# Splitting the bias, key and value loads of a chunk-band attention over two blocks of a program, and moving two state stores

## The chip, the cores and the metric

The kernel runs on one core of a Trainium2 chip. The metric is the device time of one launch in microseconds. A launch computes one whole inference step: 1024 prompt frames and 8 sample requests of 16 frames, nine tiles of 128 rows in all.

## What is computed

The step is one layer of a streaming encoder. A combined projection gives the queries, keys and values of two branches, and the gates. Branch A is a chunk-band softmax attention with a learned bias by relative distance; branch B is a retention with a recurrent state. They are merged, and a mixture of experts and an embedding follow. What the change touches is branch A for the prompt, and the updated retention states of the samples, which are outputs:

```python
def rel_bias_block(table, n_q, n_k, offset):
    dist = jnp.arange(n_q)[:, None] + offset - jnp.arange(n_k)[None, :]
    idx = jnp.clip(dist, -REL_CLIP, REL_CLIP) + REL_CLIP
    return table[:, idx].astype(F32)

def attend(q, k, v, bias, valid=None):
    s = jnp.einsum('bqhd,bkhd->bhqk', q, k).astype(F32) * (HEAD_DIM_A ** -0.5) + bias[None]
    ...
    p = jax.nn.softmax(s, axis=-1)
    return jnp.einsum('bhqk,bkhd->bqhd', p.astype(v.dtype), v)
...
    new_state = state * jnp.exp(log_g * T)[None, :, None, None] + jnp.einsum(
        'bjhd,bjhe->bhde', k * k_decay[None, :, :, None], v)
```

A prompt tile t of 128 queries sees its own 128 keys and up to 512 keys before it, so tile 0 uses one block of 128 keys, tile 1 two, and tiles 4 to 7 all five (`blocks(t)`). There are 8 heads.

## The kernel before

Everything is written out by hand: each engine has its own list of instructions, and semaphores tie them. `build` (L3112) makes two blocks of its own and one in `stage_ab`; at the end of a block all engines meet in a **barrier**. The change works around the first barrier, between the block of `stage_ab` (with `retain_samples`, L949) and the block that begins with `stage_c` (L1151).

The matmul work that does not depend on the attention is "hosted" in it (`Hosted`, L876): the gate columns of the projection, 6 panels of 512 columns for 9 tiles, which makes 54 **units** numbered u = 0 to 53. A unit is 8 slabs of 3 matmuls of 128x512 (`split_product`, L161 to L163). Its rows, 1 MiB, are loaded by `load_rows` (L913) when unit u-2 is done; its 256 KB result is evicted by ScalarE (L923) and stored (L918). Units 0 to 5 (`LEAD`, 48 slabs) run in the first block, beside the last part of the retention for the samples; unit 6 on, in the attention. There, a step n is one head of one prompt tile, n = 8t + h, and TensorE computes 6 slabs per step for n below 16 and 5 after that. A panel of the weights is 2 MiB: panel 1 is loaded whole (L893) in the first block, panel 2 in four pieces of 512 KB (L897) at n = 5, 6 and 7.

The order of DMA issues on SyncE (SP) is written in `retain_samples` (L993 to L1041) and in `stage_c` (L1244 on). Nearly all transfers of the kernel are issued there, on one queue. In the first block SP loads the kept keys `c.kT` (L1017, 9 tiles, 2.25 MiB), the values `c.vA` (L1018, 2.25 MiB) and the queries of tile 0 (L1019). Then it goes through u = 0 to 5. At u = 1 it loads the bias, 8 DMAs (L1033), each of 16 partitions x 8 heads x 640 columns, 320 KB. At u = 3 it stores four even sample states (L990, 512 KB each, through `states`). At u = 5 it waits until the even states have landed (`even_stored`), because panel 1 goes into their place, loads the panel, stores two of the odd states, and then loads the rows of unit 7. ScalarE stores the other two odd states after the eviction of unit 4. GpSimd (POOL) sets the two corners of the bias that the band excludes (L1067, L1069) when all of the bias has landed. The vector engine starts the attention with a wait for both (L1326), TensorE with a wait for keys and values (L1490).

Of the kernel before, what the change touches and what calls it, by code (L numbers as in the profile page):

```python
# [12 lines left out]
P = 128  # L13
D = 1024
KD = D // P
SEQ, DEC_B, DEC_S = 1024, 8, 16
PT = SEQ // P
NT = PT + 1
HA, HDA = 8, 64
# [929 lines left out]
def retain_samples(c, block, b):  # L949
# [8 lines left out]
    st_done = s.counter("st_done", HB)  # L958
    st_out = s.counter("st_out", DEC_B * HB)
    tables_in, states_in, even_stored, stored, bias_in = (c.sem(f"b2_{n}") for n in ("tables_in", "states_in", "even_stored", "stored", "bias_in"))  # L960
    c.kv_in, c.bias_ready = c.sem("kv_in"), c.sem("bias_ready")
    halves, raw = [c.at(R1 + 4 * 1024 * par, DEC_B // 2, HB, DV) for par in range(2)], c.at(R1 + 16 * 1024, KD, BANK)
    st = [halves[n % 2][:, n // 2] for n in range(DEC_B)]
    c.qz_in, = s.dmas("qz_in")
# [21 lines left out]
    def states(eng, par, some):  # L986
        for j in some:
            n = 2 * j + par
            eng.wait_ge(*st_out(0, 16 * par + 8 + 2 * j + 2))
            eng.dma_start(c.o["state_s"][n].rearrange("h d e -> d h e"), st[n]).then_inc(stored if par else even_stored, 16)  # L990

    @block.sync
    def _(sp):  # L993
        s.credit(sp)
# [19 lines left out]
        for stored_ in kv_stored:  # L1014
            sp.wait_ge(*stored_(NT - 1, 0))
            sp.wait_ge(*stored_(NT - 2, 1))
        sp.dma_start(c.kT, c.kT_kept).then_inc(c.kv_in, 16)  # L1017
        sp.dma_start(c.vA, c.o["v_all"].rearrange("t p n -> p t n")).then_inc(c.kv_in, 16)  # L1018
        sp.dma_start(c.qz_tiles[:, 0].rearrange("p h n -> p (h n)"), row(c.qz, 0)).then_inc(*c.qz_in.inc(0))  # L1019

        for u in range(LEAD // KD):
            if u == LEAD // KD - 1:
                sp.wait_ge(even_stored, 16 * DEC_B // 2)
                H.load(sp, 1)
                states(sp, 1, (0, 1))
            H.load_rows(sp, u + 2)
            if u < LEAD // KD - 1:
                H.store(sp, u)
            if u == 1:
                sp.wait_ge(b["state_stored"], 16)  # L1030
                sp.wait_ge(*b["kd_ready"](last))
                for q in range(DEC_B):
                    sp.dma_start(c.bias[q:P:DEC_B], bass.AP(tensor=c.skew.tensor, offset=P - 1 - q, ap=[  # L1033
                        [SKEW - DEC_B, DEC_S], [DEC_S * SKEW, HA], [1, NKB * P]])).then_inc(bias_in, 16)
            if u == 3:
                sp.wait_ge(*rb_ready(last))
                sp.dma_start(row(c.rb, NT - 1), rb.rearrange("p h n -> p (h n)")).then_inc(stored, 16)
                states(sp, 0, range(4))
# [17 lines left out]
    @block.gpsimd  # L1056
    def _(pool):
        pool.wait_ge(*proj_done(last, 4))
        nc.gpsimd.memset(qm, 0.0).then_inc(*km_ready.inc)
        pool.wait_ge(tables_in, 48)  # L1060
        for par in range(2):
            nc.gpsimd.tensor_tensor(km[:, par], kr.rearrange("p (h n) -> p h n", h=HB),
                                    kdec[:, par].unsqueeze(2).to_broadcast([P, HB, DK]), ALU.mult).then_inc(*km_ready.inc)
        pool.wait_ge(*ms_ready(last))
        nc.gpsimd.tensor_tensor(rstd, ms, c.half[:, 0:HB], ALU.pow).then_inc(*rstd_ready.inc)
        pool.wait_ge(bias_in, 16 * (P // DEC_S))
        nc.gpsimd.memset(c.bias[0:64, :, 576:], NEG).then_inc(c.bias_ready, 1)  # L1067
        pool.wait_ge(c.bias_ready, 1)
        nc.gpsimd.memset(c.bias[64:P, :, 0:64], NEG).then_inc(c.bias_ready, 1)  # L1069

    @block.vector
    def _(dve):
# [73 lines left out]


SCALE = HDA ** -0.5


def stage_c(c, block):  # L1151
# [29 lines left out]
    def blocks(t):  # L1181
        return min(t + 1, NKB)
# [61 lines left out]
    def _(sp):  # L1244
# [3 lines left out]
        def load_q(t):  # L1248
            sp.wait_ge(*s_done(t - 2))
            sp.dma_start(qz[:, t % 2].rearrange("p h n -> p (h n)"), row(c.qz, t)).then_inc(*qz_in.inc(t % 2))  # L1250

        H.store(sp, LEAD // KD - 1)
        load_q(1)

        def load_keys(n):
            sp.wait_ge(*kT_done(n - 2))
# [15 lines left out]
        for n, (t, h) in enumerate(steps):  # L1272
            if n and h == 0 and t + 1 < PT:
                load_q(t + 1)
            if n in (44, 52):
                load_keys((n - 44) // 8)
            if 8 <= n < 16:
# [39 lines left out]
    @block.gpsimd  # L1317
    def _(pool):
        nc.gpsimd.memset(zeros, 0.0).then_inc(zeroed, 1)
        nc.gpsimd.memset(cv[:, :, 2, :], 0.0).then_inc(values_padded, 1)  # L1320
        give_back(c, *past)
        F.ungated(pool)

    @block.vector
    def _(dve):
        dve.wait_ge(c.bias_ready, 2)  # L1326

        def head(t, h):
            n = blocks(t) * P
            dve.wait_ge(*s_done(t, h + 1))  # L1330
            dve.wait_ge(*p_ready(t, h - 1))
            two = lambda ap: ap.rearrange("p (a n) -> p a n", a=2)
            nc.vector.scalar_tensor_tensor(two(S[:, h % 2, 0:n]), s_halves(h, n // 2), SCALE, two(c.bias[:, h, NKB * P - n:]), ALU.mult,  # L1333
                                           ALU.add).then_inc(*s_out.inc)
# [154 lines left out]
    def _(pe):  # L1489
        pe.wait_ge(c.kv_in, 32)  # L1490

        def scores(t, f):
# [2 lines left out]
            k0, w = (t - (nb - 1)) * P, nb * P // 2  # L1495
            if f == 0:
                pe.wait_ge(*qz_in(t, t % 2))
            pe.wait_ge(*s_out(t, 2 * f))
            for part in range(2):
                for h in (2 * f, 2 * f + 1):  # L1500
# [1658 lines left out]
```

## Time and profile before

| | us |
|---|---|
| median of 3 runs | 1954.7 |
| the runs | 1951.64, 1954.7, 1957.15 |
| the profiled execution, its own time | 1951.89 |
| its span, first to last instruction | 1950.1 |
| TensorE (PE) busy | 1856.6, 95% |
| DVE, ACT, POOL busy | 1124.6, 841.5, 201.3 |

The profile is of one execution. It gives the busy time of each engine, the same in 40 slices of the span, the granted clock of TensorE, the busy share of the 16 DMA engines, and the chain of work that ended last. A busy share of a DMA window can come out above 1.00, since the packets of a transfer overlap. In the timeline a row gives the start in us, the duration, engine, line, operation and tiles; in brackets stands the idle time of the engine before it and what ended it. "SPq" rows are DMA issues of SyncE: their duration is the time of issuing, not that of the transfer.

### The profile page before, as it was taken

How to read it: one execution, taken by the hardware profiler on the slowest of the kernel's cores; microseconds unless marked ns; L12 is line 12 of the kernel's file. 1: busy time of each engine (PE TensorE's matmuls, PEld its weight loads, DVE VectorE, ACT ScalarE, POOL GpSimd, SP SyncE). 2: the span in 40 equal slices, each digit the busy share in tenths (PEclk: the TensorE clock that was granted, in tenths of full speed). 3: DMA queues.
4: the chain of work that ended last, by engine and by line, in shares of the span. 5: the costliest groups of instructions: out<-in, count | busy, mean ns of one | idle time of the engine just before them, and what ended most of it. 6: DMA issues, size and time to landing. Idle time of an engine off the chain costs nothing. (4 is left out here: it accounts for less than half of the span.)

```text
span 1950.1 us, 26441 instructions
## 1 busy us (share of the span) xinstructions
PE 1856.6 (95%) x9542; PEld 1517.9 (78%) x9542; DVE 1124.6 (58%) x1389; ACT 841.5 (43%) x1026; POOL 201.3 (10%) x235
## 2 busy tenths in 40 slices
PE   6999999998999999989999997899999999999598
PEld 5888888876777777767888886788888888888486
DVE  5344333343333445436445436689988998898674
ACT  4223000010343444435222213687778777877442
POOL 1000211120000000001322001100000000000220
PEclk9999999999999999999999998899999999999799
DMA  9656111179879766496334437599999999998762
GB/s 344 232 180 246 60 70 46 59 262 323 294 250 333 269 208 211 156 364 222 124 133 165 162 114 323 218 389 404 398 393 396 405 399 392 391 404 339 252 199 76
DMA packets 122271, 497.32 MB, mean 255 GB/s; under 512 B 17872, under 2 KB 33752, under 8 KB 99416
## 3 DMA queue, kind: packets, MB, share of 16 engines
q1 hardware_dynamic: 111360, 469.24, 64.8%
q0 software_dynamic: 7200, 18.88, 2.8%
q10 hardware_dynamic: 3640, 8.26, 1.1%
q8 instruction: 44, 0.72, 0.1%
q14 instruction: 27, 0.22, 0.0%
HBM read 411.53 MB, written 92.14 MB: 258 GB/s over the span
## 5 line engine op out<-in xcount | busy, mean ns | idle before, releaser
L2677 DVE TENSOR_TENSOR expert_w_rounded<-arena,expert_w_rounded 128x2048 fp32r<-128x2048 f32 x126 | 283.0, 2289 | 30.9 <-ACT expert_w_rounded L2612 28.9
L162 PE MATMUL psum<-expert_w_rounded,expert_x_rounded 128*128 128x512 f32 x640 | 250.0, 391 | 0.0
L2612 ACT ACTIVATE expert_w_rounded<-arena 128x2048 fp32r<-128x2048 f32 x126 | 233.9, 1911 | 0.0
L161 PE MATMUL psum<-expert_w_rounded,expert_x_rounded 128*128 128x512 f32 x504 | 202.1, 401 | 0.0
L163 PE MATMUL psum<-expert_w_rounded,expert_x_rounded 128*128 128x512 f32 x504 | 197.0, 391 | 0.0
L161 PE MATMUL psum<-host_w_rounded,host_x_rounded 128*128 128x512 f32 x432 | 177.3, 410 | 12.3 <-DMA host_x_rounded<-hx_scratch 6.8
L162 PE MATMUL psum<-host_w_rounded,host_x_rounded 128*128 128x512 f32 x432 | 171.0, 396 | 0.0
L163 PE MATMUL psum<-host_w_rounded,host_x_rounded 128*128 128x512 f32 x432 | 170.9, 396 | 0.0
L162 PEld LDWEIGHTS psum<-expert_w_rounded,expert_x_rounded 128*128 128x128 f32 x640 | 120.8, 189 | 23.4
L1333 DVE SCALAR_TENSOR_TENSOR arena<-psum,arena 128x640 f32<-128x640 f32 (+4 forms) x64 | 41.8, 653 | 167.5 <-PE psum L1502 167.5
L2612 ACT ACTIVATE first_gate_rounded<-arena 128x2048 fp32r<-128x2048 f32 x64 | 119.1, 1917 | 1.4 <-DMA arena<-w_down_e 1.4
L161 PE MATMUL psum<-b_w_rounded,b_x_rounded 128*128 128x512 f32 x288 | 115.2, 400 | 0.5 <-DVE b_w_rounded L434 0.5
L163 PE MATMUL psum<-b_w_rounded,b_x_rounded 128*128 128x512 f32 x288 | 112.3, 390 | 0.0
L162 PE MATMUL psum<-b_w_rounded,b_x_rounded 128*128 128x512 f32 x288 | 112.2, 389 | 0.0
L163 PEld LDWEIGHTS psum<-expert_w_rounded,expert_x_rounded 128*128 128x128 f32 x504 | 94.6, 188 | 20.5
L692 ACT ACTIVATE arena<-psum,arena 128x512 f32<-128x512 f32 x18 | 12.4, 689 | 224.9 <-PE psum L163 224.9
L161 PEld LDWEIGHTS psum<-expert_w_rounded,expert_x_rounded 128*128 128x128 f32 x504 | 95.2, 189 | 17.7
L161 PEld LDWEIGHTS psum<-host_w_rounded,host_x_rounded 128*128 128x128 f32 x432 | 83.0, 192 | 32.8 <-DMA host_x_rounded<-hx_scratch 9.3
L161 PE MATMUL psum<-first_gate_rounded,expert_x_rounded 128*128 128x512 f32 x264 | 104.4, 396 | 4.3 <-DVE expert_x_rounded L2683 4.3
L163 PE MATMUL psum<-first_gate_rounded,expert_x_rounded 128*128 128x512 f32 x264 | 103.9, 394 | 0.0
L161 PE MATMUL psum<-a_w_rounded,a_x_rounded 128*128 128x512 f32 x216 | 85.6, 396 | 17.5 <-DVE a_w_rounded L591 17.5
L163 PEld LDWEIGHTS psum<-host_w_rounded,host_x_rounded 128*128 128x128 f32 x432 | 82.6, 191 | 18.2
(321 smaller groups left out, 3832.0 us busy)
## 6 DMA issues: line engine op xcount, KB each, us to landing
arena<-w_gate_e SPq DMA_DIRECT2D x32, 2048.0 KB, 13.6
arena<-w_up_e SPq DMA_DIRECT2D x32, 2048.0 KB, 14.1
arena<-w_down_e SPq DMA_DIRECT2D x32, 2048.0 KB, 13.2
host_x_rounded<-hx_scratch SPq DMA_DIRECT2D x54, 1024.0 KB, 5.5
y_scratch<-arena SPq DMA_DIRECT2D x49, 512.0 KB, 11.9
z_scratch<-arena SPq DMA_DIRECT2D x54, 256.0 KB, 5.8
arena<-w_in SPq DMA_DIRECT2D x6, 2048.0 KB, 11.7
arena<-x_all SPq DMA_DIRECT2D x18, 512.0 KB, 6.0
```

The costliest lines, as they stand in the source:

```text
L161: nc.tensor.matmul(out, x_hi, w_hi, start=first, stop=False)
L162: nc.tensor.matmul(out, x_hi, w_lo, start=False, stop=False)
L163: return nc.tensor.matmul(out, x_lo, w_hi, start=False, stop=last)
L692: nc.scalar.activation(v[:, b, h * BANK:(h + 1) * BANK], ps[:, 2 + h, :], ACT.Copy, scale=row_rstd[:, b:b + 1]).then_inc(*bv_out.inc)
L1333: nc.vector.scalar_tensor_tensor(two(S[:, h % 2, 0:n]), s_halves(h, n // 2), SCALE, two(c.bias[:, h, NKB * P - n:]), ALU.mult, ALU.add).th ...
L2612: nc.scalar.activation(c.exact(his[0 if last_down(n, e) else n][:, half, :]), halves[b][n][:, half, :], ACT.Copy).then_inc(*w_hi_ready[n].inc)
L2677: nc.vector.tensor_tensor(c.exact(raw), raw, c.high(his[0 if last_down(n, e) else n][:, half, :]), ALU.subtract).then_inc(*w_lo_ready[n].inc)
```

## The change

It makes four edits.

- Keys and values are loaded in two parts by `load_kept`. The first block loads tiles 0 to 3 (`EARLY` = 4), 1 MiB each. Step n = 10 of the attention loads keys of tiles 4 to 8 (1.25 MiB) and values of tiles 4 to 7 (1 MiB). Tile 8 of the values is no longer loaded. TensorE waits for the second part at prompt tile 4.
- The bias is loaded in two parts by `load_bias`. The first block loads the last 256 of 640 columns (from `NEAR` = 384), 8 DMAs of 128 KB. The other 384 columns come one DMA per step at n = 0 to 7, 192 KB each.
- The two odd state stores of SP go behind the barrier, after the queries of tile 1.
- POOL's second corner is set in the second block, when all of the bias is in. DVE waits for the first corner at the start of the attention and for the second at prompt tile 2.

```diff
+    c.odd_states = states
...
-        sp.dma_start(c.kT, c.kT_kept).then_inc(c.kv_in, 16)
-        sp.dma_start(c.vA, c.o["v_all"].rearrange("t p n -> p t n")).then_inc(c.kv_in, 16)
+        load_kept(c, sp, 0, EARLY)
...
                 H.load(sp, 1)
-                states(sp, 1, (0, 1))
...
-                    sp.dma_start(c.bias[q:P:DEC_B], bass.AP(tensor=c.skew.tensor, offset=P - 1 - q, ap=[
-                        [SKEW - DEC_B, DEC_S], [DEC_S * SKEW, HA], [1, NKB * P]])).then_inc(bias_in, 16)
+                    load_bias(c, sp, q, NEAR, NKB * P)
...
-        pool.wait_ge(bias_in, 16 * (P // DEC_S))
+        pool.wait_ge(bias_in, 16 * DEC_B)
         nc.gpsimd.memset(c.bias[0:64, :, 576:], NEG).then_inc(c.bias_ready, 1)
-        pool.wait_ge(c.bias_ready, 1)
-        nc.gpsimd.memset(c.bias[64:P, :, 0:64], NEG).then_inc(c.bias_ready, 1)
...
+EARLY, NEAR = 4, (NKB - 2) * P
+
+
+def load_kept(c, eng, t0, t1):
+
+    eng.dma_start(c.kT[:, :, t0 * P:t1 * P], c.kT_kept[:, :, t0 * P:t1 * P]).then_inc(c.kv_in, 16)
+    t1 = min(t1, PT)
+    eng.dma_start(c.vA[:, t0:t1], c.o["v_all"][t0:t1].rearrange("t p n -> p t n")).then_inc(c.kv_in, 16)
+
+
+def load_bias(c, eng, q, n0, n1):
+
+    eng.dma_start(c.bias[q:P:DEC_B, :, n0:n1], bass.AP(tensor=c.skew.tensor, offset=P - 1 - q + n0, ap=[
+        [SKEW - DEC_B, DEC_S], [DEC_S * SKEW, HA], [1, n1 - n0]])).then_inc(c.bias_in, 16)
...
         load_q(1)
+        c.odd_states(sp, 1, (0, 1))
...
+            if n < DEC_B:
+                load_bias(c, sp, n, 0, NEAR)
+            if n == 10:
+                load_kept(c, sp, EARLY, NT)
...
         nc.gpsimd.memset(cv[:, :, 2, :], 0.0).then_inc(values_padded, 1)
+        pool.wait_ge(c.bias_in, 32 * DEC_B)
+        pool.wait_ge(values_padded, 1)
+        nc.gpsimd.memset(c.bias[64:P, :, 0:64], NEG).then_inc(c.bias_ready, 1)
...
-        dve.wait_ge(c.bias_ready, 2)
+        dve.wait_ge(c.bias_ready, 1)
...
+            if (t, h) == (2, 0):
+                dve.wait_ge(c.bias_ready, 2)
...
+                if t == EARLY:
+                    pe.wait_ge(c.kv_in, 64)
```

How this moves the issues on SP is seen at two places. The first is SP around the barrier, from the load of panel 1 (`w_in`, L893) on. L913 loads the rows of a unit, L918 stores a unit's result, L436 is the end of the first block. Before:

```order
L893 DMA arena<-w_in 128x8x512
L990 DMA state_s<-arena 128x4x256 x2
L913 DMA host_x_rounded<-hx_scratch 128x2048
L436 UNCONDITIONAL_BRANCH
L1243 UNCONDITIONAL_BRANCH
L918 DMA z_scratch<-arena 128x512
L1250 DMA arena<-qz_scratch 128x1024
L913 DMA host_x_rounded<-hx_scratch 128x2048
```

Now:

```order
L893 DMA arena<-w_in 128x8x512
L913 DMA host_x_rounded<-hx_scratch 128x2048
L436 UNCONDITIONAL_BRANCH
L1256 UNCONDITIONAL_BRANCH
L918 DMA z_scratch<-arena 128x512
L1263 DMA arena<-qz_scratch 128x1024
L990 DMA state_s<-arena 128x4x256 x2
L1160 DMA arena<-bias_skew_scratch 16x8x384 x2
L913 DMA host_x_rounded<-hx_scratch 128x2048
```

The two stores have left the place ahead of the rows of unit 7 and the barrier, and stand with two bias loads ahead of the rows of unit 8 (the last L913).

The second place is SP in the attention, from the rows of unit 14 on, where the late keys and values come in. L1278 (now L1296) is a 17 KB bias load for the samples. Before:

```order
L1278 DMA arena<-bias_skew_scratch 16x272 x2
L913 DMA host_x_rounded<-hx_scratch 128x2048
L918 DMA z_scratch<-arena 128x512
L1278 DMA arena<-bias_skew_scratch 16x272
L913 DMA host_x_rounded<-hx_scratch 128x2048
```

Now:

```order
L1296 DMA arena<-bias_skew_scratch 16x272 x2
L913 DMA host_x_rounded<-hx_scratch 128x2048
L918 DMA z_scratch<-arena 128x512
L1153 DMA arena<-kT_scratch 128x4x640
L1155 DMA arena<-v_all 128x4x512
L1296 DMA arena<-bias_skew_scratch 16x272
L913 DMA host_x_rounded<-hx_scratch 128x2048
```

2.25 MiB now stand between the rows of unit 14 and those of unit 15.

## Rows read from the trace of the kernel before

**Rows 1.** The page: span, slices of PE and DMA, end of the chain by line

```profile
span 1950.1 us, 26441 instructions
...
PE   6999999998999999989999997899999999999598
...
DMA  9656111179879766496334437599999999998762
...
PE psum L161 11%; PE psum L163 10%; PE psum L162 10%; PE psum L2730 1%; PE psum L2746 1%; DMA arena<-y_scratch,arena 1%; DMA arena<-w_down_e 0%; DMA y_scratch<-arena 0%; PE psum L3097 0%; DVE expert_w_rounded L2677 0%; DVE arena L2973 0%; ACT arena L2320 0%; PE psum L2392 0%; DVE arena L2966 0%; POOL arena L2937 0%
```

**Rows 2.** Busy time by window, around the barrier and in early attention

```profile
core 0: us, PE busy (x) PEld busy (x) DVE busy (x) ACT busy (x) POOL busy (x), PEclk, DMA share, GB/s
425.00:500.00 75.00, 60.58 (x338) 44.80 (x338) 24.59 (x60) 9.90 (x14) 7.12 (x8) 0.89 1.02 347
...
520.00:540.00 20.00, 20.00 (x105) 15.69 (x104) 4.48 (x16) 5.04 (x16) 0.00 (x0) 1.00 0.93 332
```

**Rows 3.** Timeline of TensorE: start us, duration us, line, tiles [idle before <-releaser]

```profile
470.66 0.50 PE L161 MATMUL psum<-host_w_rounded,host_x_rounded 128*128 128x512 f32 x1 [3.10 <-DMA host_x_rounded<-hx_scratch]
...
474.88 0.40 PE L163 MATMUL psum<-host_w_rounded,host_x_rounded 128*128 128x512 f32 x1
...
491.55 1.11 PE L1502 MATMUL psum<-arena 64*128 64x64 f32 x8 [6.82 <-SPq L62]
492.59 0.79 PE L161 MATMUL psum<-host_w_rounded,host_x_rounded 128*128 128x512 f32 x1
...
495.19 0.39 PE L161 MATMUL psum<-host_w_rounded,host_x_rounded 128*128 128x512 f32 x1
...
499.77 0.50 PE L161 MATMUL psum<-host_w_rounded,host_x_rounded 128*128 128x512 f32 x1 [0.32 <-DMA host_x_rounded<-hx_scratch]
...
506.34 0.39 PE L161 MATMUL psum<-host_w_rounded,host_x_rounded 128*128 128x512 f32 x1
...
552.69 0.48 PE L161 MATMUL psum<-host_w_rounded,host_x_rounded 128*128 128x512 f32 x1
...
597.82 0.50 PE L161 MATMUL psum<-host_w_rounded,host_x_rounded 128*128 128x512 f32 x1 [1.66 <-DMA host_x_rounded<-hx_scratch]
```

**Rows 4.** Timeline of SP's DMA issues, 425 to 555 us

```profile
466.52 0.33 SPq L913 DMA_DIRECT2D host_x_rounded<-hx_scratch  x1
...
468.11 7.54 SPq L990 DMA_DIRECT2D state_s<-arena  x4
479.32 0.35 SPq L913 DMA_DIRECT2D host_x_rounded<-hx_scratch  x1
...
482.17 0.39 SPq L893 DMA_DIRECT2D arena<-w_in  x1
482.60 4.88 SPq L990 DMA_DIRECT2D state_s<-arena  x2
487.52 3.12 SPq L913 DMA_DIRECT2D host_x_rounded<-hx_scratch  x1
...
538.33 0.35 SPq L913 DMA_DIRECT2D host_x_rounded<-hx_scratch  x1
...
545.55 0.33 SPq L913 DMA_DIRECT2D host_x_rounded<-hx_scratch  x1
```

**Rows 5.** Timeline of ScalarE, its last eviction before the barrier

```profile
484.76 0.69 ACT L923 ACTIVATE arena<-psum,arena 128x512 f32<-128x512 f32 x1 [4.75 <-PE psum L163]
```

**Rows 6.** Issue to landing: bias, 447 to 453 us; ACT's stores, 479 to 481; rows, 499 to 560

```profile
L1033 SPq DMA_DIRECT2D arena<-bias_skew_scratch x8: 600/604/643, 447.9 to 452.5; - x8
...
DMA to landing us min/median/max: 7.8/11.0/15.8
...
state_s<-arena ACTq DMA_DIRECT2D x2, 512.0 KB, 11.0
...
L913 SPq DMA_DIRECT2D host_x_rounded<-hx_scratch x10: 328/333/352, 499.5 to 558.4; - x10
...
DMA to landing us min/median/max: 5.2/5.3/6.4
```

More of the change, by code:

```diff
@@ L960, in retain_samples @@
     tables_in, states_in, even_stored, stored, bias_in = (c.sem(f"b2_{n}") for n in ("tables_in", "states_in", "even_stored", "stored", "bias_in"))
-    c.kv_in, c.bias_ready = c.sem("kv_in"), c.sem("bias_ready")
+    c.kv_in, c.bias_in, c.bias_ready = c.sem("kv_in"), bias_in, c.sem("bias_ready")
     halves, raw = [c.at(R1 + 4 * 1024 * par, DEC_B // 2, HB, DV) for par in range(2)], c.at(R1 + 16 * 1024, KD, BANK)
```

## The prediction

> **What bounds the kernel now.** I read the page first. TensorE is busy nine tenths or more in nearly every slice, and the chain that ended last is TensorE's three product lines [rows 1]. So time is gained only where TensorE stands idle or slow, and the change touches one such place: the slices from 425 to 500 us. The table by windows shows there 60.6 us of TensorE in 75, a granted clock of 0.89, and a DMA share of 1.02: the queue is full over the whole stretch [rows 2]. Third, TensorE's timeline. There are two waits. At 470.66 it has waited 3.10 us for the rows of unit 4. At 491.55 it has waited 6.82 us for SP at the barrier [rows 3]. Each also costs clock. After the first, the 12 products from 470.66 to 474.88 take 4.22 us from the first start to the last; at the 0.226 us of undisturbed products (11 x 0.226 = 2.5) that is **1.7 us lost**. After the second, six products take 2.6 us from 492.59 to 495.19 instead of 1.4, **1.2 us lost**. The granted clock was at the lower of its two levels, 1.2 instead of 2.4 GHz. After waits of 0.32 and 1.66 us nothing comparable is seen [rows 3]. Fourth, SP's issues: before the barrier it spends 4.88 us on two state stores and 3.12 us on the rows of unit 7, because the queue takes no more [rows 4], while ScalarE's last eviction had ended at 485.45 [rows 5].
>
> In all that is 3.1 + 1.7 + 6.8 + 1.2 = 12.8 us. The question is how much of it the queue lets go.
>
> **What the queue carries.** Its pace is worked out between two landings that TensorE waits for: the rows of unit 4 at 470.6 and those of unit 7 at 499.7 [rows 3]. Between them land 10.25 MiB: results of units 2, 3 and 4 (0.75), rows of units 5, 6 and 7 (3), a branch B tile (0.5), eight state stores, two of them from ScalarE (4), and panel 1 (2). That is 29.1 us, or **2.84 us per MiB**. On an empty queue a unit's rows land in 5.3 us [rows 6], so 2.5 us are fixed. The bias is slower. The eight DMAs were issued from 447.9 to 452.5, the first landed after 7.8 us and the last after 15.8, so 12.6 us for seven of 320 KB: 1.8 us each, twice the pace above [rows 6].
>
> **Edits 1 and 2, the first block.** The queue loses 2.5 MiB of keys and values, and the bias shrinks from 8 x 1.8 to about 8 x 0.7 us. Both lie ahead of the rows of unit 4, so these land without a wait. TensorE starts unit 4 at 467.6 and keeps its clock: it is 3.1 + 1.7 = 4.8 us earlier, and ends unit 5 at 479.9 instead of 484.7.
>
> **Edit 3, the barrier.** SP now has only the panel and the rows of unit 7 to issue there. The panel waits for the even states. The rows of unit 5 are issued at 466.52 [rows 4], now into an empty queue, which works from 469.0. Ahead of the end of the even states stand 1 + 0.25 + 0.5 + 2 = 3.75 MiB, and up to 1 MiB of ScalarE's stores is served beside them (ScalarE's took 11.0 us against 5.3 for a lone load [rows 6]). They land between 479.7 and 482.5. SP reaches the barrier a microsecond later; before, 0.9 us lay between SP's end and TensorE's start (490.64 to 491.55 [rows 3, 4]). So TensorE goes on between 481.5 and 484.3. That would be 7 to 10 us of gain.
>
> **What is late next.** The rows of unit 7. They stand behind 9.0 MiB counted from unit 5's rows on, themselves included: 1 (unit 5), 0.25, 0.5, 2 (even states), 1 (unit 6), 0.25, 1 (ScalarE's states), 2 (panel), 1. That is 25.6 us, so they land at 469.0 + 25.6 = **494.6**, against 499.7. TensorE would need them near 490. Of the 7 to 10 us it keeps 5.1.
>
> Then the rows of unit 8. The two odd stores have only moved from ahead of unit 7's rows to ahead of unit 8's, and the first two bias pieces are put there too. 0.25 + 0.5 (queries) + 1 (odd states) + 1 = 2.75 MiB is 7.8 us. A piece of 192 KB costs 1.8 x 192/320 = 1.1 us, two 2.2 us. They land at 494.6 + 7.8 + 2.2 = **504.6**. Unit 8 began at 506.34 before [rows 3], so **1.7 us** are left. TensorE waits here for between 1.7 and 3.4 us, which lies between a wait without loss of clock and one with 1.7 us of loss; I take half, 0.85.
>
> The remaining six bias pieces come one per step. From 520 to 540 us the DMA share is 0.93 already, with panel 2 [rows 2], so there is little room, but the rows of a unit have 1 to 2 us to spare (5.3 us against 6.5 or so per unit). I take zero. For the late keys and values the rows of unit 14 were issued at 538.33 and land at 543.6; 0.25 MiB of result and 2.25 MiB are 7.1 us, so 550.7. The rows of unit 15 land 2.8 us later, at 553.5, and unit 15 began at 552.69 [rows 3, 4]. Cost **0.7 us**.
>
> At nothing: the wait of DVE for the second corner at tile 2, some 30 us after the last bias piece; TensorE's at tile 4, over 100 us after the load; POOL's memset, half a microsecond on an idle engine, with nothing behind it that is due; eight more issues on SP, 0.6 us each, in a queue with pauses of several us between units.
>
> **Sum.** 1.7 - 0.85 - 0.7 = 0.15 us faster: 1951.9 becomes 1951.7 for the profiled execution. The runs' median is 2.8 us above that execution, so I predict 1954.5. After unit 15 nothing that the change moves is left.
>
> **Two rules of the Trainium skill.** The trace shows the bias loads, contiguous runs of 2560 bytes, at half the queue's pace [rows 6]. The page "DMA: Bandwidth & Descriptors", Specifications, gives 512 bytes as the smallest transfer for line rate; by it a piece of 192 KB would cost 0.5 us and not 1.1, and unit 8's rows would land 1.2 us earlier. The trace disagrees, for runs five times that long. The same page, How a descriptor splits into AXI transactions, says that a run that does not start on 256 bytes costs one transaction more. Cutting such a run in two makes 5 + 7 transactions of 11, which speaks against this change: a 192 KB piece would be 1.15 us and unit 8 0.1 us later. No row here shows it.
>
> **The rivals.**
> - *No wait at unit 8* (0.15). The rows of unit 8 come in time, because the pace is better once the small state stores are through, and the bias costs what its bytes cost elsewhere. Then 5.1 - 0.7 = 4.4 us stay: 1950.3. For it: the pace was measured over a stretch with many small stores. Against it: two of these stores are still ahead of unit 8.
> - *The queue is not what decides* (0.10). The rows of unit 7 come by 489, the barrier's gap shrinks to about 1.7 us, too short to cost clock: 4.8 + 5.2 + 1.2 - 0.7 = 10.5 us, 1944.2. It needs 9.0 MiB in 20 us, 2.2 us per MiB, where no row shows better than 2.8.
> - *Slower: a bias DMA costs by its count and not by its bytes* (0.06). Each is 128 runs, and the half-size ones would take 1.8 us like the whole ones. The change doubles their number and puts eight where the rows of units are just in time. Unit 8 is 1.4 us later (gain 0.3) and loses 1.7 of clock. From 520 to 540 us there is 7% or 1.4 us of room for three pieces of 5.4 us: 4.0 lost, and clock once, 1.7. With 0.7 at unit 15 that is 7.8 us slower, 1962.5. It decides from some 1.6 us per piece on. For it: the 1.8 us at half pace have no cause that a row shows. Against it: the 512 KB stores, of as many runs times four, took 1.4 us.
> - *It does not do what it says* (0.02): the corner or the late keys hold up tile 2 or 4. The distances above speak against it.
>
> **How the numbers follow.** The forecast has 0.67. With the bounds (bias piece 0.5 or 1.8 us, clock lost or not, 2.65 or 2.84 us per MiB) it goes from 4 us faster to 3 slower, and the three runs lie within 3.1 us of their median. So 1950 to 1958 is its own, and to leave out no more than 2 in 10 I take **1947.5 to 1959**. A measurement here can tell 0.3%, 5.9 us, from no change. Faster by more: the second rival, a third of the first, and 0.03 of the forecast by the spread of runs, 0.18. Slower by more: 0.07. Within: 0.75.
>
> **What would show it.** In the changed profile: no wait at unit 4; SP's barrier wait under 5 us instead of 6.8; in its place waits for the unit rows (host_x) at units 7 and 8, and a small one at unit 15; unit 8 starting between 503 and 506. Wrong would be no wait at unit 7, or unit 7's rows landing before 491, or bias pieces that land over 1.5 us apart on a full queue.

## The result and the profile after

| | before | changed |
|---|---|---|
| median of 20 runs each, us | 1955.58 | 1958.32 |
| lowest to highest, us | 1949.73 to 1959.08 | 1954.87 to 1964.74 |
| the profiled execution: its time, its span | 1951.89, 1950.1 | 1955.64, 1953.8 |
| ratio to the kernel before, 95% interval | | 1.0018 (1.0011 to 1.0025) |

The changed kernel is slower by about 3.5 us by the ratio (the medians are 2.7 us apart). That is under the 0.3% named in the prediction, but its interval leaves 1 out. The forecast was 1954.5, with a range of 1947.5 to 1959: the time lies in the range, 3.8 us from the forecast, and it moved the other way from the 0.15 us that the sum gave.

The page of the changed kernel, the lines that answer to [rows 1]:

```profile
span 1953.8 us, 26452 instructions
...
PE   6999999998999999989999997899999999999598
...
DMA  9656111178979856596334437699999999998762
```

At this resolution nothing has happened. The table by windows, for the stretch of [rows 2] and the one behind it:

```profile
425.00:500.00 75.00, 64.84 (x362) 48.10 (x361) 25.59 (x64) 11.10 (x18) 6.70 (x7) 0.91 0.89 298
500.00:560.00 60.00, 53.55 (x267) 41.02 (x266) 21.22 (x59) 22.28 (x57) 0.52 (x1) 0.97 0.86 303
```

From 425 to 500 us TensorE is busy 64.8 us where it was 60.6, and has done 362 instructions where it had done 338; the DMA share fell from 1.02 to 0.89. So the first block is relieved, as meant. From 500 to 560 us TensorE is busy 53.6 us of 60. In the kernel before, TensorE has 60.00 us there, with 312 instructions against 267, and the DMA share is 0.72 against 0.86:

```profile
500.00:560.00 60.00, 60.00 (x312) 47.36 (x312) 22.28 (x62) 24.20 (x62) 0.00 (x0) 1.00 0.72 250
```

The gain of the first stretch, and more, is spent there. The timeline of TensorE says where (compare [rows 3]):

```profile
484.78 0.96 PE L1527 MATMUL psum<-arena 64*128 64x64 f32 x8 [4.97 <-SPq L62]
486.11 0.80 PE L161 MATMUL psum<-host_w_rounded,host_x_rounded 128*128 128x512 f32 x1 [0.37 <-DMA host_x_rounded<-hx_scratch]
...
495.15 0.50 PE L161 MATMUL psum<-host_w_rounded,host_x_rounded 128*128 128x512 f32 x1 [0.63 <-DMA host_x_rounded<-hx_scratch]
...
503.87 0.50 PE L161 MATMUL psum<-host_w_rounded,host_x_rounded 128*128 128x512 f32 x1 [2.00 <-DMA host_x_rounded<-hx_scratch]
...
531.85 0.50 PE L161 MATMUL psum<-host_w_rounded,host_x_rounded 128*128 128x512 f32 x1 [1.35 <-DMA host_x_rounded<-hx_scratch]
...
545.13 0.50 PE L161 MATMUL psum<-host_w_rounded,host_x_rounded 128*128 128x512 f32 x1 [0.27 <-DMA host_x_rounded<-hx_scratch]
...
555.69 0.50 PE L161 MATMUL psum<-host_w_rounded,host_x_rounded 128*128 128x512 f32 x1 [2.84 <-DMA host_x_rounded<-hx_scratch]
```

These are the restart after the barrier and units 6, 7, 8, 12, 14 and 15. Where each unit starts, read from such rows in both traces:

| unit | before | changed | difference | TensorE's wait ahead of it, changed |
|---|---|---|---|---|
| 4 | 470.66 | 467.33 | -3.3 | none (was 3.10) |
| 5 | 479.12 | 474.22 | -4.9 | none |
| barrier | 491.55 | 484.78 | -6.8 | 4.97 (was 6.82) |
| 6 | 492.59 | 486.11 | -6.5 | 0.37 |
| 7 | 499.77 | 495.15 | -4.6 | 0.63 |
| 8 | 506.34 | 503.87 | -2.5 | 2.00 |
| 12 | 532.58 | 531.85 | -0.7 | 1.35 |
| 14 | 545.36 | 545.13 | -0.2 | 0.27 |
| 15 | 552.69 | 555.69 | **+3.0** | 2.84 |
| 16 | 558.25 | 562.90 | **+4.7** | none, slow products in unit 15 |
| 25 | 628.52 | 634.23 | +5.7 | 0.63 |
| 53 | 887.32 | 894.54 | +7.2 | 1.3 (as before) |
| end | 1950.07 | 1953.79 | +3.7 | |

After the wait at unit 15, products follow each other 0.4 us or more apart for a while, then 0.23 us again. The granted clock falls to the lower of its two levels (its mean is 0.61 from 555.7 to 560 us), and 1.7 us went (unit 15 lasts 7.2 us; before, 5.56):

```profile
559.31 0.63 PE L162 MATMUL psum<-host_w_rounded,host_x_rounded 128*128 128x512 f32 x1
559.74 0.56 PE L163 MATMUL psum<-host_w_rounded,host_x_rounded 128*128 128x512 f32 x1
560.14 0.40 PE L161 MATMUL psum<-host_w_rounded,host_x_rounded 128*128 128x512 f32 x1
```

SP's issues around the barrier and around the late keys and values (compare [rows 4]):

```profile
482.31 0.39 SPq L893 DMA_DIRECT2D arena<-w_in  x1
482.74 1.18 SPq L913 DMA_DIRECT2D host_x_rounded<-hx_scratch  x1
...
487.65 1.01 SPq L990 DMA_DIRECT2D state_s<-arena  x2
488.71 5.39 SPq L1160 DMA_DIRECT2D arena<-bias_skew_scratch  x2
494.55 0.49 SPq L913 DMA_DIRECT2D host_x_rounded<-hx_scratch  x1
...
541.35 0.63 SPq L1153 DMA_DIRECT2D arena<-kT_scratch  x1
542.02 0.73 SPq L1155 DMA_DIRECT2D arena<-v_all  x1
542.79 2.87 SPq L1296 DMA_DIRECT2D arena<-bias_skew_scratch  x1
545.70 0.49 SPq L913 DMA_DIRECT2D host_x_rounded<-hx_scratch  x1
```

The 4.88 us of two state stores and 3.12 us of unit 7's rows have shrunk to 1.18 us. The time stands behind the barrier now: the first of the two bias pieces took 4.6 us to issue, since the queue took no more. The 17 KB issue behind the late keys and values took 2.87 us in this execution; in the five other profiles with the same loads at this place it took 0.50 to 0.67 us, so the bytes ahead of it do not explain it alone. Issues from 541 to 543.5 us, KB each, and median us from issue to landing, and the rows of unit 15, issued at 545.70, with who waited for them:

```profile
arena<-kT_scratch SPq DMA_DIRECT2D x1, 1280.0 KB, 9.1
arena<-v_all SPq DMA_DIRECT2D x1, 1024.0 KB, 11.1
...
aT_scratch<-arena ACTq DMA_DIRECT2D x1, 256.0 KB, 7.0
```

```profile
  PE psum L161: 2.8, 1
...
DMA to landing us min/median/max: 9.9/9.9/9.9
```

The rows of unit 15 take 9.9 us where such a load takes 5.3 on an empty queue [rows 6]. They land at 555.6.

### The profile page after: what moved, and what is told of

Its sections match the earlier page's. It is cut to its first block and busy times, and to the rows that moved or that the text cites. A ratio compares the mean times of both kernels' runs of the same rounds, so it can differ in the third digit from the quotient of the medians.

```text
span 1953.8 us, 26452 instructions
## 1 busy us (share of the span) xinstructions
PE 1855.7 (95%) x9542; PEld 1516.3 (78%) x9542; DVE 1124.6 (58%) x1389; ACT 841.1 (43%) x1026; POOL 201.5 (10%) x235
```

## The experiments

Each kernel is the changed one with one edit more, unless said otherwise. "Unit 17" and "unit 53" are the differences of their starts to the first profile of the kernel before (565.69 and 887.32). Theory K: the late keys and values at n = 10 cost the time, at unit 15. Theory B: the bias pieces in the attention do. Theory Q: the queue from 470 to 560 us is full, and a transfer moved within it only moves a wait.

| kernel | ratio to before (95%) | median | wait at 15 | unit 17 | unit 53 |
|---|---|---|---|---|---|
| the change | 1.0018 (1.0011 to 1.0025) | 1958.32 | 2.8 | +4.7 | +7.2 |
| values later | 0.9988 (0.9978 to 0.9998) | 1953.47 | 0 | +2.1 | +1.5 |
| keys, values back | 0.9977 (0.9964 to 0.9990) | 1951.59 | 0 | +2.0 | +3.7 |
| the same again | 0.9997 (0.9985 to 1.0010) | 1953.26 | 0 | -0.1 | +0.7 |
| bias back | 0.9989 (0.9975 to 1.0003) | 1952.55 | 4.1 | +4.4 | +4.0 |
| the same again | 0.9997 (0.9985 to 1.0009) | 1954.43 | 2.7 | +4.8 | +8.0 |
| state stores back | 1.0013 (1.0001 to 1.0025) | 1957.52 | 2.8 | +3.9 | +5.9 |
| rows first | 1.0014 (1.0002 to 1.0026) | 1957.90 | 2.3 | +4.9 | +7.3 |
| spread | 1.0012 (0.9999 to 1.0025) | 1958.78 | 0 | +6.4 | +8.1 |
| the change again | 1.0009 (0.9997 to 1.0021) | 1957.41 | 1.6 | +4.2 | +5.6 |
| keys, values and bias back | 0.9995 (0.9983 to 1.0006) | 1951.69 | 0 | +0.6 | -0.6 |
| the best | 0.9985 (0.9974 to 0.9996) | 1949.87 | 0 | +1.0 | -1.4 |
| the kernel before, once more | | 1947.24 | 0 | -0.1 | -0.7 |

The median of the kernel before moves too, from 1953.14 to 1955.58 between the groups of runs, so ratios are compared and not medians. The ratio of one and the same kernel moves too, by 0.0008 to 0.0020 between its two groups. The version called spread has no wait at unit 15, but one of 2.3 us at unit 14.

### Values later (kept_apart)

```diff
             if n == 10:
-                load_kept(c, sp, EARLY, NT)
+                sp.dma_start(c.kT[:, :, EARLY * P:NT * P], c.kT_kept[:, :, EARLY * P:NT * P]).then_inc(c.kv_in, 16)
+            if n == 13:
+                sp.dma_start(c.vA[:, EARLY:PT], c.o["v_all"][EARLY:PT].rearrange("t p n -> p t n")).then_inc(c.kv_in, 16)
```

> The changed kernel with the late values moved from step 10 to step 13, the late keys left at step 10. Theory Q (one queue served in order: 2.25 MiB in one go stand ahead of the rows of unit 15): the wait of 2.84 us at unit 15 falls below 1 us and its clock loss (about 1.7 us) goes; units 4 to 14 start as in the changed kernel; the time is 4 to 5 us under the changed kernel's, 1953.5 to 1955. Rival B (the time is lost to the price of the many small bias pieces, or to the new waits for corner and keys): unit 15 still waits over 2 us, and the time stays within 1 us of the changed kernel's 1958.3.

Its TensorE timeline, units 12 and 15, and its waits from 500 to 640 us (line waited for: us in total, times, longest):

```profile
533.00 0.61 PE L161 MATMUL psum<-host_w_rounded,host_x_rounded 128*128 128x512 f32 x1 [1.73 <-DMA host_x_rounded<-hx_scratch]
```

```profile
554.75 0.48 PE L161 MATMUL psum<-host_w_rounded,host_x_rounded 128*128 128x512 f32 x1
```

```profile
PE psum L161 <- DMA host_x_rounded<-hx_scratch: 5.1, 4, 2.1
```

Unit 15 starts without a wait; in the changed kernel TensorE waits 10.1 us seven times in that window, here 5.1 us four times. The wait at unit 12 stayed and here cost clock as well, which is why unit 17 is still 2.1 us late. Units 4 to 14 had been expected to start as in the changed kernel; unit 14 came 2.3 us later. The ratio lies 0.0030 or 5.9 us under that of the change and 0.0021 under that of the change again, and its interval does not touch that of the first. 5.9 us are more than the 2.8 + 1.7 = 4.5 us at unit 15, and the two profiles differ by only 2.6 us at unit 17. Theory K holds in that the wait goes when the values move and the time falls with it; that all of the 5.9 us are its own is not shown.

### Keys and values back (kept_back, kept_back_2)

```diff
         load_kept(c, sp, 0, EARLY)
+        load_kept(c, sp, EARLY, NT)
...
-            if n == 10:
-                load_kept(c, sp, EARLY, NT)
```

> The changed kernel with all keys and values loaded in the first block again (in the same two parts, one right behind the other; tile 8 of the values still left out). Theory Q: no wait at unit 15. Ahead of unit 4's rows stand 2.25 MiB or 6.4 us more, of which 2.7 us fill the pause that the queue has there in the changed kernel: unit 4's rows land at 468.2 instead of 464.5, a wait of about 0.9 us. The time is 3 to 4 us under the changed kernel's, about 1954.5 to 1955.5. Rival B: unit 15 waits as in the changed kernel, the time is 1959 or more.

> The kernel of kept_back again (all keys and values in the first block, bias split, odd states behind the barrier), since its median was 0.9977 of the kernel before with a profile 3.8 us longer than the first profile of before. If late keys and values are the main cost of the change, the ratio to the kernel before is again under 1.0000 and at least 0.002 under the changed kernel's 1.0018 and 1.0009; the second profile shows no wait at units 4 and 15, unit 17 within 2.5 us of the kernel before. If the first ratio was luck, it is 1.000 or above.

The rows of unit 4, issued at 458.4, from issue to landing, with the late part loaded in the first block:

```profile
DMA to landing us min/median/max: 6.4/6.4/6.4
```

In the changed kernel it is 6.2. So the extra 2.25 MiB in the first block was **free**, where I had expected a wait of 0.9 us: there is no wait at unit 4 in either profile. Unit 15 waits in neither. The second profile did not lose clock at unit 12 and is level with the kernel before at unit 17. The two ratios are 0.0041 and 0.0021 under that of the change, and 0.0032 and 0.0012 under that of the change again. For the second, at least 0.002 under both had been expected, so this was met against the one and missed against the other. The first profile is also a slow execution of its group (1955.75 us, median 1951.59). Keys and values did not make unit 4 late by themselves; with the whole bias behind them they did (below, the whole bias without them leaves 1.1 to 1.8 us of wait, the two together 3.1 to 4.1).

### Bias back (bias_back, bias_back_2)

```diff
-                    load_bias(c, sp, q, NEAR, NKB * P)
+                    load_bias(c, sp, q, 0, NKB * P)
...
-            if n < DEC_B:
-                load_bias(c, sp, n, 0, NEAR)
...
-        pool.wait_ge(c.bias_in, 32 * DEC_B)
+        pool.wait_ge(c.bias_in, 16 * DEC_B)
```

> The changed kernel with the bias loaded whole in the first block again. Theory Q: the wait at unit 4 is back with some 3 us and 1.7 us of clock; the waits at unit 8 (2.00) and unit 12 (1.35) shrink to under 1 us each, the one at unit 15 stays over 2 us; time within 2 us of the changed kernel's. Rival B (the bias pieces are what costs): the time falls by 3 us or more.

> The kernel of bias_back again, since its timed runs (median 1952.55, 5.8 us under the changed kernel's) and its one profile (4.1 us of wait at unit 15, span 0.8 us under the changed kernel's) disagree. If the profile is typical, the median comes out at 1956.5 to 1959. If the bias pieces in the attention are a cost of their own in most executions, the median is again under 1954, and the wait at unit 15 in this second profile is smaller than 2 us or one before it is gone.

The rows of unit 15 in the first of the two, who waited for them, and how long they took:

```profile
  PE psum L161: 4.1, 1
...
DMA to landing us min/median/max: 11.5/11.5/11.5
```

Unit 4 waited 1.1 and 1.8 us. Unit 8 was 1.2 us earlier than in the change in the first, unit 12 waited 0.2 us instead of 1.35. All of that lead went into a longer wait at unit 15, and at unit 17 both profiles stand where the change stands (+4.4, +4.8 against +4.7). By that the bias pieces cost nothing. At unit 4 the wait was 1.1 us and without loss of clock, where 3 us and a loss had been expected. The ratios say otherwise: both lie under that of the change, by 0.0029 and 0.0021 (0.0020 and 0.0012 under the change again), and the first median fell by 5.8 us, as rival B had it; the second, 1954.43, lies between what the two theories had said. So taking out the bias pieces helps the time nearly as much as taking out the late keys and values, and the one does not rule out the other. The two profiles do not show how: they are the slower kind of their groups (1954.84 us with a median of 1952.55, and 1959.73 us, the slowest of 12). Whether a typical execution of this kernel waits at unit 15 no run shows, and the difference stays open.

### State stores back (states_back)

```diff
                 H.load(sp, 1)
+                states(sp, 1, (0, 1))
...
-        c.odd_states(sp, 1, (0, 1))
```

> The changed kernel with SP's two odd state stores ahead of unit 7's rows and the barrier again. Theory Q: the stores only change places with unit 7's rows in a full queue. Unit 7's rows land 2.8 us later and the wait at the barrier is longer by some 2 to 3 us; unit 8's rows land at the same time as in the changed kernel, so from unit 8 on nothing differs by more than 1 us; time within 1 us. Rival (the barrier is what costs): 3 to 5 us slower than the changed kernel.

The restart after the barrier:

```profile
488.46 1.12 PE L1527 MATMUL psum<-arena 64*128 64x64 f32 x8 [9.21 <-SPq L62]
```

TensorE waits 9.2 us at the barrier instead of 5.0, and restarts 3.7 us later. At unit 8 both stand at the same place (503.96 against 503.87), and at unit 17 they are 0.8 us apart. Theory Q holds: the move of the state stores turns a barrier wait into waits for unit rows and has no worth at unit 8 or later.

### Rows first (rows_first)

```diff
+            H.load_rows(sp, u + 2)
                 H.load(sp, 1)
-            H.load_rows(sp, u + 2)
```

(The `+` line stands ahead of the branch that loads panel 1, the `-` line behind it.)

> The changed kernel with one swap on SP before the barrier: the rows of unit 7 are issued ahead of panel 1. Theory Q (the queue is full from 466 to 504 us, and a swap in it only moves a wait): unit 7's rows land near 490 instead of 495.1, its wait of 0.6 us goes and unit 7 starts near 492; unit 8's rows land as before the swap, 503.8, so its wait grows from 2.0 to over 3 us and unit 8 starts within 1 us of 503.9; from there nothing changes, time within 1.5 us of the changed kernel's. Rival (the order around the barrier is what costs): unit 8 starts 3 us earlier and the time falls as much.

```profile
503.72 0.79 PE L161 MATMUL psum<-host_w_rounded,host_x_rounded 128*128 128x512 f32 x1 [5.30 <-DMA host_x_rounded<-hx_scratch]
...
555.94 0.67 PE L161 MATMUL psum<-host_w_rounded,host_x_rounded 128*128 128x512 f32 x1 [2.29 <-DMA host_x_rounded<-hx_scratch]
```

Unit 7 starts at 491.83 with no wait, 3.3 us ahead of the change. Unit 8 then waits 5.3 us and starts at 503.72, where it started anyway (503.87). It then loses some 2 us of clock, of which 0.5 are left at unit 12 (532.31 against 531.85): the change waits 1.35 us there, this kernel not at all. The same as the state stores: unit 8's rows are set by the bytes ahead of them.

### Spread

```diff
+            H.load_rows(sp, u + 2)
...
-        c.odd_states(sp, 1, (0, 1))
...
+            if n in (1, 3):
+                c.odd_states(sp, 1, (n // 2,))
+            for q in BIAS_AT.get(n, ()):
+                load_bias(c, sp, q, 0, NEAR)
+            if n in (11, 12):
...
+            if n in (13, 14):
...
```

`BIAS_AT` puts the bias pieces at n = 2, 3, 4, 8, 9, 9, 10, 10; the late values come in halves at n = 11 and 12, the keys at 13 and 14.

> The changed kernel with the swap of rows_first, the two odd state stores at steps 1 and 3, the bias pieces at steps 2, 3, 4, 8, 9, 9, 10, 10, and the late keys and values in four parts of 0.5 to 0.75 MiB at steps 11 to 14. Nothing but panel 1, a result and the queries stands then ahead of unit 8's rows. Theory Q: unit 7 starts near 492, unit 8's rows land near 500 and unit 8 starts at 500 to 501, 6 us ahead of the kernel before; no wait at units 12 to 17 over 1 us; unit 17 starts at 560 to 561.5, 4 to 5.5 us ahead of the kernel before, and the time is 1950 to 1952. Rival (the DMA work in the attention costs wherever it is put): unit 17 starts less than 1.5 us ahead of the kernel before, the time is 1954 or more.

ScalarE and TensorE at the split of panel 1:

```profile
509.35 4.27 ACT L902 ACTIVATE host_w_rounded<-arena 128x512 fp32r<-128x512 f32 x8 [9.56 <-DMA state_s<-arena]
```

```profile
514.50 0.45 PE L1542 MATMUL psum<-arena 128*128 128x128 f32 x1 [6.43 <-ACT arena L1436]
```

Missed, by my own doing. ScalarE's rounding of panel 1 (L902) waits for all four odd stores. In the change it starts at 502.5, right behind an eviction. With the second store at n = 3 it starts at 509.35, after 9.56 us of idle time for `state_s`, and TensorE waits 6.43 us for ScalarE. After it the clock is low (0.52 from 514.5 to 520 us). Unit 8 was 5.2 us ahead of the kernel before, unit 12 is 3.9 us behind it. Unit 15 has no wait, as theory K says, but unit 14 waits 2.29 us: its rows took 9.4 us, behind the last piece of panel 2, the queries and three bias pieces that I had put at n = 8 and 9. So this version does not test the spreading of the late loads alone, and its +6.4 us have two causes.

### The change again (after_again)

> The changed kernel itself on the same chip as the three above, for a comparison side by side: 1957 to 1959.5, with waits at units 8, 12 and 15 as in its first profile.

```profile
503.02 0.50 PE L161 MATMUL psum<-host_w_rounded,host_x_rounded 128*128 128x512 f32 x1 [2.02 <-DMA host_x_rounded<-hx_scratch]
...
533.32 0.50 PE L161 MATMUL psum<-host_w_rounded,host_x_rounded 128*128 128x512 f32 x1 [2.04 <-DMA host_x_rounded<-hx_scratch]
...
556.88 0.50 PE L161 MATMUL psum<-host_w_rounded,host_x_rounded 128*128 128x512 f32 x1 [1.59 <-DMA host_x_rounded<-hx_scratch]
```

The same waits, at units 8, 12 and 15, but the clock fell after the first two and not after the last. Unit 17 is at +4.2 (first profile +4.7).

### Keys, values and bias back (both_back)

The edits of kept_back and of bias_back together. Of the change only the state stores and the second corner are left.

> The changed kernel with keys, values and bias all in the first block again: of the change only the two odd state stores behind the barrier and the second corner in the attention are left (and tile 8 of the values left out). Theory Q: unit 4's rows land as in bias_back, near 468, up to 3 us later by the 2.25 MiB: a wait of 1 to 3 us there; the queue from 466 us on is that of bias_back, so unit 8 starts 2 to 4 us ahead of the kernel before, and no bias piece, keys or values come after: unit 17 starts 2 to 4 us ahead too, time 1951.5 to 1953.5. If the state stores behind the barrier gain nothing by themselves, it is 1955 or more.

Missed: unit 4 waits 4.1 us again, the barrier 1.4 instead of 6.8, unit 7 4.5 us, and unit 8 is +0.6. Two to four microseconds ahead were expected at unit 17; it is +0.6. The time, 1951.69, lies in the expected 1951.5 to 1953.5 by luck: the kernel before was at 1953.14 in this group, and the ratio, 0.9995 (0.9983 to 1.0006), shows no difference. So no worth of moving the state stores is seen from the kernel before either.

### The best (best)

```diff
         load_kept(c, sp, 0, EARLY)
+        load_kept(c, sp, EARLY, NT)
...
+            H.load_rows(sp, u + 2)
...
-            H.load_rows(sp, u + 2)
...
+BIAS_AT = (2, 3, 4, 9, 10, 11, 12, 13)
...
-            if n < DEC_B:
-                load_bias(c, sp, n, 0, NEAR)
-            if n == 10:
-                load_kept(c, sp, EARLY, NT)
+            if n in BIAS_AT:
+                load_bias(c, sp, BIAS_AT.index(n), 0, NEAR)
```

> All keys and values in the first block (as kept_back), the rows of unit 7 ahead of panel 1 (as rows_first), SP's two odd states right behind the barrier as in the changed kernel, and the far bias pieces one per step at steps 2, 3, 4, 9, 10, 11, 12 and 13, that is neither ahead of unit 8's rows nor beside the pieces of panel 2. Theory Q: no wait at unit 4; unit 7 starts near 492; unit 8's rows land 2.2 us earlier than in rows_first, near 501.5, and unit 8 starts there; no wait over 1 us at units 12 and 15; unit 17 starts 2.5 to 4.5 us ahead of the kernel before; time 1951 to 1953. If the loss is not in the queue ahead of the units' rows, unit 17 starts less than 1 us ahead and the time is 1955 or more.

```profile
502.69 0.71 PE L161 MATMUL psum<-host_w_rounded,host_x_rounded 128*128 128x512 f32 x1 [2.91 <-DMA host_x_rounded<-hx_scratch]
...
531.46 0.50 PE L161 MATMUL psum<-host_w_rounded,host_x_rounded 128*128 128x512 f32 x1 [0.54 <-DMA host_x_rounded<-hx_scratch]
```

It comes out faster than both kernels: 0.9985 (0.9974 to 0.9996), about 2.9 us under the kernel before. It is one group of 12 runs, and the kernel of kept_back, with 0.9977 in its first group, had 0.9997 in its second; so the gain is not confirmed. Unit 8 was expected at 501.5 and came at 502.69, with 1.7 us of clock lost after it. The lead of 3.6 us at unit 8 is gone at unit 17 (+1.0 where 2.5 to 4.5 us ahead were expected), in a clock loss and small waits at units 12, 13 and 14. At unit 53 it is 1.4 us ahead. So if this version is better, it is not through the lead that it was made for.

### The kernel before, once more (before_copy)

> The kernel before, profiled once more, to see how far one profile of it stands from another: waits at unit 4, barrier and units 20 and 21 within 0.5 us of the first profile's, start of unit 53 within 1.5 us of 887.3, and the span up to 5 us longer, since the first profile's 1951.9 was at the low end of the timed runs (medians 1954.9 to 1955.6).

Two of these missed: unit 20 has no wait, where 0.88 us stood in the first profile, and the span is 4.7 us shorter and not longer. Units 8 and 17 are 0.1 us from the first profile, unit 53 is 0.7 us ahead, the end 4.7 us. Between unit 53 and the end, 4.0 us have come from somewhere else; the vector engine's instructions, set side by side one by one in the two traces, put 3.4 us of them between 1210 and 1300 us. The window 1210 to 1230 us in the first profile of the kernel before, and in this one:

```profile
1210.00:1230.00 20.00, 18.63 (x78) 14.89 (x77) 7.39 (x16) 9.51 (x19) 5.39 (x6) 0.83 0.76 298
```

```profile
1210.00:1230.00 20.00, 17.17 (x88) 13.53 (x87) 9.61 (x16) 9.93 (x20) 5.41 (x6) 1.00 0.82 316
```

The granted clock was 0.83 in one and 1.00 in the other, and 78 products stand against 88. The changed kernel has 1.00 there too and makes good 3.5 us between 1210 and 1300 us, which is how its +7.2 us at unit 53 became +3.7 at the end. So the end of one profile says little about 3 us here. The unit starts up to unit 17 say more, and the ratios of many runs say most.

## Why the prediction was right and where it was wrong

**Right: the first block, the barrier, units 7 and 8.** Every step up to unit 8 came within 1.1 us. Unit 4 at 467.33 (predicted 467.6), without a wait or loss of clock. The restart at 484.78, half a microsecond outside 481.5 to 484.3. The rows of unit 7 landing at 495.1 (494.6) and those of unit 8 at 503.8 (504.6), so the queue's pace of 2.84 us per MiB held over 35 us. Unit 8 was 2.5 us earlier where 1.7 had been worked out. The 0.85 us of clock was not lost there in this execution; in the second profile all of 1.7 us was. That is the pair of cases that the half stood for. The bound of 2.65 us per MiB in the range comes from no row, and nothing hung on it.

**Wrong: "Cost 0.7 us" at unit 15.** This is the step that failed. In place of 0.7 us it cost, from unit 14's -0.2 to unit 16's +4.7, **4.9 us**. The sum for unit 15's rows began from 543.6 and reached 553.5; they landed at 555.6. The 2.1 us are in three parts. Unit 14's rows landed at 545.1 and not at 543.6: 1.5. They were issued 0.7 us earlier than in the kernel before and took 7.5 us and not 5.3, since the queue still had work ahead of them. The bias pieces are not needed for that: in bias_back and bias_back_2, which have none here, the same rows took 7.0 and 8.0 us. In the second execution of the change, where TensorE was 2.4 us late by then, they took 5.2. So rows that a lead asks for earlier can meet a queue that is still busy. From there to the landing of the late values it took 8.0 us for 2.5 MiB (7.1 predicted): 0.9. The third is a gain of 0.3: unit 15's rows took 2.5 us more, not 2.8. In the stretch of the overrun ScalarE stored 256 KB on its own queue (the aT_scratch row above), a transfer that my sum had left out; at the pace above it is 0.7 us.

Then I had set the landing (553.5) against the start of unit 15 in the kernel before (552.69), a delay of 0.8 us (the prediction has 0.7). With the 0.2 us of lead that were left at unit 14, unit 15 would have started at 552.46; it started at 555.69, 3.2 us later (the profile lists 2.84 of them as idle, since it lets the last product end at 552.85). And I had added no clock to it, though for unit 8 I had priced a wait of that size with a possible 1.7. It cost 1.7: 3.2 + 1.7 are the 4.9 us.

Six profiles have the 2.25 MiB at n = 10 in one go, and all six wait 1.6 to 4.1 us at unit 15 and stand at +3.9 to +4.9 at unit 17. The six profiles of changed kernels with the keys and values elsewhere do not wait there; apart from the one that I spoilt at panel 1 they stand at -0.1 to +2.1. In the terms of the sum: 2.5 us ahead at unit 8, 0.7 at unit 12, 0.2 at unit 14, and 4.7 behind at unit 16.

**Wrong: "I take zero" for the last six bias pieces.** They stand with panel 2's pieces and the queries in a queue that had 7% of room. The rows of unit 12 took 8.2 us instead of 5.4, and TensorE waited 1.35 us (2.0 in the second execution; 1.7, 1.9 and 1.2 where only the keys and values were placed otherwise, with and without a loss of clock). My argument compared 5.3 us with 6.5 us of a unit, and an empty queue is not what those rows met. The price that shows is 1.6 us of the lead (unit 9 to unit 12, -2.3 to -0.7). Where the clock fell as well it was more: in kept_back 3.6 us from unit 9 to unit 13 (-1.6 to +2.0), all of which is still there at unit 17. In the kernel with the bias back, unit 13 then waited 1.0 us, so a part would have gone anyway. With the late keys and values behind it, it made no difference by unit 17; the ratios of bias_back say that somewhere it does.

**Wrong: "After unit 15 nothing that the change moves is left."** Nothing that it moves is left, but TensorE loses another 2.5 us from unit 17 to unit 53 (1.4 in the second profile), mostly at waits that were there before: 2.20 us at unit 21 instead of 1.66, 1.4 at unit 50 instead of 0.8, and 0.63 at unit 25 where there was none. In the kernel before once more, the same stretch gained 0.6. The kernels without the wait at unit 15 have anything from -2.4 to +1.7 here. Why an execution that is 4.7 us late has more such waits was not tested.

**The rivals.** *A bias DMA costs by its count* named the right outcome by a mechanism that did not occur. The eight near pieces, 128 KB each, in the changed kernel:

```profile
L1160 SPq DMA_DIRECT2D arena<-bias_skew_scratch x8: 599/606/623, 448.0 to 452.6; - x8
...
DMA to landing us min/median/max: 4.9/5.0/5.5
```

Issued over 4.6 us and landed 5.0 us later each, they came as fast as SP issued them, 0.65 us apart; the whole ones had come 1.8 us apart. So two fifths of the bytes cost no more than 0.65 us and the count does not decide. *The queue is not what decides* fell: unit 7's rows landed at 495.1, not by 489. *No wait at unit 8* fell with its 2.00 us. That the change would not do what it says fell as well; no wait for the corner or the late keys shows up.

**The rule of the Trainium skill.** The smallest transfer for line rate ("DMA: Bandwidth & Descriptors", Specifications) would have made unit 8's rows land at 503.4, my own price at 504.6; they landed at 503.8. Between the second odd store (499.7) and these rows lie 4.1 us for 1 MiB and two bias pieces, so at 2.84 per MiB some 0.65 us per piece, an estimate between the 0.5 of the page and my 1.1. The trace's DMA packets, read by size, bear it out: the 1536-byte packets of these pieces take 81 ns on average, and eight on each of the 16 DMA engines make 0.65 us. For the small price in the attention the rule was the nearer; in the first block it was not. There the 2560-byte packets of the whole loads take 201 ns, 1.6 us per DMA, and the 1024-byte packets of the near pieces 79 ns, 0.63 us, while the 1024-byte packets of the odd state stores take 46. So my price by bytes at half the queue's pace was right for the loads of the first block and wrong for those of the attention, and the length of the run is not what decides. What does, no run here shows.

## What to carry to other kernels

A queue that is full (from 466 to 504 us here) has no free place within it: state stores moved behind a barrier, or rows moved ahead of a panel, changed which wait TensorE stood in and left unit 8 where it was. Ask of each moved transfer what the queue carries in the next few units at its new place, in bytes and from both issuing engines, and begin the sum from the landing that these make late and not from one on an empty queue. A lead is not kept by itself: the rows are asked for earlier, while the queue may still be busy with what stands ahead of them. And look first whether the place that it came from was short at all: 2.25 MiB of keys and values were free in the first block and cost 4.9 us at unit 15 in the attention.

## What the runs showed of the hardware

- **The clock after a wait is not a matter of the wait's length alone.** Waits for rows of 1.35, 1.59, 1.66, 2.00, 2.09, 2.20 and 2.29 us left it at 2.4 GHz; waits of 1.73, 1.90, 2.00, 2.02, 2.04, 2.29, 2.51 and 2.84 us were followed by some 8 slow products and a loss of 1.5 to 1.7 us. At unit 8, 2.00 us cost nothing in one execution of the changed kernel and 2.02 us cost 1.7 in the other; at unit 21 it was the other way round, 2.20 and nothing, 2.00 and 1.6. In this kernel a wait for rows of 1.7 to 2.3 us is priced at anything from its own length to 1.7 more.
- **The same kernel's end varies by nearly 5 us between two profiles** (1950.1 and 1945.4), while unit 17 differs by 0.1. 3.4 us of it come between 1210 and 1300 us, where the granted clock differs (0.83 and 1.00 from 1210 to 1230 us).
- **A full queue shows in SP's issue times.** A bias issue that takes 0.6 us took 4.6 us behind panel 1, unit 7's rows, the queries and two state stores. It is a sign and not a measure: behind 2.25 MiB of keys and values one issue took 2.87 us in one profile and 0.50 to 0.67 us in five others.
- **DMA packets of one size can differ in time by nearly two.** 1024-byte packets of bias loads took 79 ns at 448 to 458 us, those of state stores 46 ns at 494 to 499 us, both in the changed kernel.
